# Second block: inverse norms of the keys computed early, and one low weight half carried over a seam of the expert passes

## The chip, the cores and the metric

One core of one Trainium2 chip runs the whole program. The metric is the device time of one execution in microseconds (us), as the median of the runs. A profiled execution of the kernel before stands beside it; all times of single instructions come from that execution and are counted from its first instruction.

## What is computed

Two transformer blocks over 256 tokens of width 1024. The first is not touched. The second normalizes the latent and 256 context tokens, multiplies both by one wide matrix, and feeds three mixers: a gated recurrence ("hgrn"), an RWKV-7 recurrence and a neighbourhood attention. A router then picks experts, and a mixture of 32 experts ends the block. What the change touches is this part of the RWKV mixer and the experts:

```python
def prep(p):
    p = p + (centred_shift(p) - p) * mu
    r, k, v, wdf, wdb, adf, adb, gd = jnp.split(p, list(RWKV_SPLITS), axis=-1)
    kk = hd(k * kk_scale)
    kk = kk / jnp.maximum(jnp.sqrt(jnp.sum(kk * kk, axis=-1, keepdims=True)), 1e-12)
    for d, (wd, ad) in enumerate(((wdf, adf), (wdb, adb))):
        w = -jax.nn.softplus(-(w0[d] + jnp.tanh(wd) @ w_up[d])) - 0.5
        decay = jnp.exp(-jnp.exp(w))
        ...
        dirs.append((hd(decay), hd(k_d), hd(a) * kk))
...
for gi in range(N_GROUPS):
    hid = silu(einsum('nd,edf->nef', h, w_gate[gi])) * einsum('nd,edf->nef', h, w_up[gi])
    y = y + einsum('nef,efd->nd', hid * comb[:, gi, :, None], w_down[gi])
```

## The kernel before

The weights of all large products are split in two parts: ScalarE (ACT) copies a "high" part, VectorE (DVE) subtracts it for the "low" part, and TensorE (PE) does three products for one.

**Second projections.** `second_projections` is one section, with a barrier at each end. Every engine runs one fixed list of instructions, in order. The list comes from generators that yield planned times; `in_turn` always takes the generator with the least planned time (of equals the one named first). The planned times serve only for this order. On the chip an engine runs its list as fast as its semaphores let it.

The input matrix comes in 31 pieces: f (6), vg (4), rw (9, in the order 6, 7, 2, 3, 4, 5, 0, 1, 8), nq, nk and nv (4 each). An f or rw piece gives one unit of output. The four pieces of vg, nq, nk or nv add up to several units, one for each tile of 128 tokens (nq has the tiles 2 and 3 only). The units take PSUM banks 0 to 3 in a ring, in the order of `names`: unit u uses bank u mod 4, and `units.open` makes PE wait until unit u-4 is read out (`units.close`). Four slots hold split pieces, so the high part of piece p waits for the products of piece p-4.

Beside these pieces run nine doubling levels of the hgrn recurrence (`levels_*`, through ACT, DVE, PE and GpSimd (POOL)), then the products that weigh the values (L2707, semaphore `weighed`), the low-rank gates of RWKV (`low_*`, banks 6 and 7), and the keys (`keys_*`). `t_weigh` is the planned time 131.0 of the weighing. In planned times relative to it:

- DVE (`keys_dve`): key times scale and its square (L2480, L2482) at 1.3; four prefix scans (L2488) at 3.6 to 4.2; low part of nv piece 0 at 4.5; the logs of direction 0 (L2498 to L2501) at 4.6 and of direction 1 (L2498 to L2506) at 5.6; low part of nv piece 1 at 10.2; maximum, reciprocal (L2512) and product (L2515) at 10.5 and 11.0; low part of nv piece 2 at 15.9; direction 0's last steps (L2521 to L2527) at 16.0; low part of nv piece 3 at 21.6; direction 1's at 22.0.
- ACT: high part of nv piece 0 at 3.3; square roots of the norms (L2459) at 6.0; copy of nk tile 0 out of PSUM (L197) at 7.3; exponentials of direction 0 (L2464) at 7.5; copy of nk tile 1 at 8.75; high part of nv piece 1 at 9.0; exponentials of direction 1 at 9.5; copies of nk tiles 2 and 3 at 10.2 and 11.6; high parts of nv pieces 2 and 3 at 14.7 and 20.4.
- PE: products of nk piece 3 at 5.6, the two sums over heads (L2443) at 5.7, products of nv piece 0 at 11.3. Its four tiles open the banks of nk's tiles 0 to 3.
- POOL (`keys_pool`): a product for each direction (L2534) once the scaled keys and that direction's exponentials are there.

**Experts.** `passes` handles a number of groups of experts: once with three groups, then once in a loop (`nc.Fori`) for the last group, then a short last stage writes the output. Each call ends with barriers. A pass has 48 halves of weights. `split(i + AHEAD)` makes the parts three halves ahead, so three halves of the next pass are split before the barrier, also after the last pass. The first work of DVE in a pass is `gated_sum` (L4186), whose split feeds the products back to the tokens (L4191) after half 1.

Of the kernel before, what the change touches and what calls it, by code (L numbers as in the profile page):

```python
# [2211 lines left out]
def second_projections(core, I, k, fv, masks, consts, mod, x, X, attended, keys, ycat, coming):  # L2212
# [8 lines left out]
    with ExitStack() as mem, core.section() as sem:  # L2221
# [33 lines left out]
        for name, i, *_ in pieces.rows:  # L2255
            if name in ("f", "rw"):
                names.append((name, i))
            elif i == 0:
                names += [(name, t) for t in tiles[name]]
        units = Units(core, sem, "sec", 4, names)  # L2260
# [142 lines left out]
        def attended_reads(eng, queue, parity):  # L2403
# [8 lines left out]
        up_here, low, low_read, gate_read = sem("up_here"), sem("low"), sem("low_read"), sem("gate_read")  # L2412
        kk_own, kk_summed, kk_rooted, scanned, key_own, key_exp, key_done, key_pool = (sem(n) for n in (
            "kk_own", "kk_summed", "kk_rooted", "scanned", "key_own", "key_exp", "key_done", "key_pool"))
        logs_made, keys_made = (3, 7), 10

# [3 lines left out]
        def low_pe(pe):  # L2420
# [24 lines left out]
        def low_act(act):  # L2445
# [6 lines left out]
            for t in range(TT):  # L2452
                yield t_weigh + 1.5 + 0.05 * t
                act.wait_ge(low, 9 + t)
                nc.scalar.activation(gt[:, t, :], low_bank(t)[:, 0:A_W], ACT.Copy).then_inc(gate_read, 1)
            for hp in range(2):
                yield t_weigh + 6.0 + 0.05 * hp
                act.wait_ge(kk_summed, hp + 1)
                nc.scalar.activation(kn[:, hp], low_bank(hp), ACT.Sqrt).then_inc(kk_rooted, 1)  # L2459
            for d in range(2):  # L2460
# [6 lines left out]
        def keys_dve(dve):  # L2467
# [7 lines left out]

            for hp in range(2):
                yield t_weigh + 1.3 + 0.1 * hp
                dve.wait_ge(weighed, TT)
                units.read(dve, ("rw", 2 + hp))
                V.tensor_scalar(kk[:, hp], X[:, 2 + hp, :], fv["kk_scale"][:, hp:hp + 1], None, ALU.mult).then_inc(kk_own, 1)  # L2480
                dve.wait_ge(kk_own, 2 * hp + 1)
                V.tensor_tensor(kn[:, hp], kk[:, hp], kk[:, hp], ALU.mult).then_inc(kk_own, 1)  # L2482
            for d in range(2):
                for hp in range(2):
                    yield t_weigh + 3.6 + 0.4 * d + 0.2 * hp
                    dve.wait_ge(low_read, 2 * d + hp + 1)
                    dve.wait_ge(out_own, 6)
                    V.tensor_tensor_scan((rt, k2)[d][:, d, hp], consts["chunk_start"], sw[:, d, hp], 0.0, ALU.mult, ALU.add)\  # L2488
                        .then_inc(scanned, 1)
            for d in range(2):  # L2490
                c = [a[:, d].rearrange("p h t -> p (h t)").rearrange("p (c n) -> p c n", n=RW_CHUNK) for a in (kt, k2, rt, sw)]
# [24 lines left out]
            assert own == keys_made  # L2516
            for d in range(2):
# [331 lines left out]
        with nc.Block(no_gpsimd_drain=True) as block:  # L2849
# [23 lines left out]
            @block.scalar  # L2873
            def _(act):
                in_turn(arrived(act), final_act(act), norms[1][2](act), context_act(act), pieces.high_parts(nc, act), bound_act(act), gate_act(act),
                        values_act(act), levels_act(act), shift_act(act), bent_act(act),
                        attended_reads(nc.scalar, act, 1), low_act(act))
# [720 lines left out]
RAW = 4  # L3598
# [542 lines left out]
def experts(core, k, hT, h_tok, weights, tile_d, tile_i, x, g_row, out, m):  # L4141
# [69 lines left out]

    def passes(n_tiles, slots_of, groups_of):

        with core.stage(*names) as (
# [8 lines left out]
            def _(sp):  # L4223
                groups = groups_of(sp)
                sp.dma_start(key[:, :], slots_of(0)).then_inc(key_here, 16)
                for u in range(RAW, n_units):
                    t = u // len(plan)
                    if t and u % len(plan) == RAW:
                        sp.wait_ge(picked, t)
                        sp.dma_start(key[:, :], slots_of(t)).then_inc(key_here, 16)  # L4230
                    if 2 * (u - RAW) + 2 > AHEAD:
                        sp.wait_ge(low, 2 * (u - RAW) + 2 - AHEAD)
                    fetch(sp, u, groups[t]).then_inc(landed[u % RAW], 16)
                for u in range(n_units, n_units + RAW):
                    sp.wait_ge(low, 2 * (u - RAW) + 2 - AHEAD)
                    sp.sem_clear(landed[u % RAW])
                    fetch(sp, u, groups[n_tiles]).then_inc(next_landed[u % RAW] if u % RAW < 2 else landed[u % RAW], 16)

            @block.tensor
            def _(pe):  # L4240
# [9 lines left out]
                for i in range(n_all):  # L4250
                    t, (u, h) = i // n_halves, halves[i % n_halves]
                    kind, e = plan[u]
                    g = PER_GROUP * t + e
                    if i >= AHEAD:
                        pe.wait_ge(low, i + 1 - AHEAD)
                    w = [halved(i, which)[1] for which in range(2)]
# [149 lines left out]
    certain = GROUPS - 1  # L4406
    passes(certain, lambda t: tile_d[t + 1], lambda sp: list(range(GROUPS)))
    tiles = nc.values_load(tile_i[0:1, TILES + 1:TILES + 2], min_val=GROUPS, max_val=TILES)

    with nc.Fori(certain, tiles, 1) as tile:  # L4410
        passes(1, lambda t: tile_d[tile + 1],
               lambda sp: [sp.value_load(tile_i[0:1, bass.ds(tile + n, 1)], min_val=0, max_val=GROUPS - 1) for n in range(2)])

# [283 lines left out]
```

## Time and profile before

| what | value |
|---|---|
| median of 3 runs | 2022.44 us (2021.68 to 2023.82) |
| profiled execution, its own time | 2018.09 us |
| span of that execution, first to last instruction | 2016.3 us |
| PE busy / DVE busy / ACT busy | 91% / 80% / 54% of the span |
| mean granted TensorE clock | 0.97 of full speed |

A busy share is an average over many stages. What matters for one edit is which wait ends last in its own section, so the rows below are mostly from the timeline of the engines in two stretches: 1092 to 1187 us (second half of the second projections) and the two barriers behind the expert passes (1858 to 1862 us and 2004 to 2007 us).

### The profile page before, as it was taken

What the parts mean: (1) busy time and instruction counts of PE and PEld (TensorE: products, weight loads), DVE (VectorE), ACT (ScalarE), POOL (GpSimd) and SP (SyncE); (2) the same over time, 40 slices, a digit from 0 to 9 for tenths busy, and PEclk for the clock granted to TensorE, in tenths of its full rate; (3) what the DMA queues carried; (4) which work ended last, traced back from release to release, by engine and by line L of the source; (5) the groups of instructions that cost most, each with busy time, mean ns of one, the idle gap of its engine ahead of it and who ended that gap; (6) DMA issues with size and microseconds to landing.
All of it is one profiled execution on the core that took longest, in us unless ns stands there. A gap on an engine that the chain in (4) does not pass through costs nothing. (4 is left out here: it accounts for less than half of the span.)

```text
span 2016.3 us, 31666 instructions
## 1 busy us (share of the span) xinstructions
PE 1830.6 (91%) x12866; PEld 1562.5 (77%) x12866; DVE 1610.4 (80%) x2113; ACT 1090.9 (54%) x1316; POOL 145.0 (7%) x151
## 2 busy tenths in 40 slices
PE   2989989998989989999899968997999999999998
PEld 2876769997866769997777657876788788787886
DVE  6778888987788888987579487557888888988887
ACT  2643636653653637562565333125677677776775
POOL 0000000000000000000056047300000000000000
PEclk9989999999999999999999987998899999999999
DMA  7667766656567757556522100006599899898997
GB/s 282 208 222 242 256 226 252 233 205 225 198 217 244 260 189 289 219 196 242 182 83 64 61 12 15 19 16 247 191 372 375 316 377 375 318 373 316 349 381 292
DMA packets 158288, 460.54 MB, mean 228 GB/s; under 512 B 11072, under 2 KB 13760, under 8 KB 155584
## 3 DMA queue, kind: packets, MB, share of 16 engines
q1 hardware_dynamic: 158144, 458.52, 63.7%
q8 instruction: 103, 1.69, 0.3%
q14 instruction: 41, 0.34, 0.1%
HBM read 457.43 MB, written 1.05 MB: 227 GB/s over the span
## 5 line engine op out<-in xcount | busy, mean ns | idle before, releaser
L217 DVE TENSOR_TENSOR me_wlow<-me_w,me_whigh 128x2048 fp32r<-128x2048 f32 (+1 forms) x203 | 451.5, 2247 | 77.5 <-ACT me_whigh L212 77.1
L212 ACT ACTIVATE me_whigh<-me_w 128x2048 fp32r<-128x2048 f32 (+1 forms) x203 | 380.3, 1885 | 116.9 <-PE ps L225 107.2
L223 PE MATMUL ps<-me_whigh,me_xhigh 128*128 128x512 f32 x512 | 204.0, 398 | 5.1 <-PEq L124 3.1
L225 PE MATMUL ps<-me_whigh,me_xlow 128*128 128x512 f32 x528 | 206.9, 392 | 0.0
L223 PE MATMUL ps<-up_xhigh,ffn_whigh 128*128 128x256 f32 x704 | 199.8, 284 | 2.6 <-DVE ffn_wlow L217 1.5
L224 PE MATMUL ps<-me_wlow,me_xhigh 128*128 128x512 f32 x512 | 200.5, 392 | 0.0
L224 PE MATMUL ps<-up_xlow,ffn_whigh 128*128 128x256 f32 x704 | 199.2, 283 | 0.0
L225 PE MATMUL ps<-up_xhigh,ffn_wlow 128*128 128x256 f32 x704 | 199.2, 283 | 0.0
L217 DVE TENSOR_TENSOR ffn_wlow<-ffn_w,ffn_whigh 128x2048 fp32r<-128x2048 f32 (+1 forms) x72 | 149.3, 2110 | 42.4 <-ACT ffn_whigh L212 42.3
L217 DVE TENSOR_TENSOR mix_wlow<-mix_w,mix_whigh 128x1024 fp32r<-128x1024 f32 (+2 forms) x116 | 140.0, 1210 | 21.8 <-ACT mix_whigh L212 21.7
L212 ACT ACTIVATE ffn_whigh<-ffn_w 128x2048 fp32r<-128x2048 f32 (+1 forms) x72 | 123.2, 1760 | 43.1 <-PE ps L225 43.1
L212 ACT ACTIVATE mix_whigh<-mix_w 128x1024 fp32r<-128x1024 f32 (+2 forms) x116 | 120.3, 1047 | 44.0 <-DMA mix_w<-w_mix 22.3
L223 PEld LDWEIGHTS ps<-up_xhigh,ffn_whigh 128*128 128x128 f32 x704 | 135.1, 192 | 3.3 <-issue 3.3
L223 PE MATMUL ps<-mix_whigh,mix_xhigh 128*128 128x512 f32 (+1 forms) x320 | 131.5, 411 | 5.8 <-DVE mix_sq L1717 2.8
L224 PEld LDWEIGHTS ps<-up_xlow,ffn_whigh 128*128 128x128 f32 x704 | 135.1, 192 | 0.0
L225 PEld LDWEIGHTS ps<-up_xhigh,ffn_wlow 128*128 128x128 f32 x704 | 135.1, 192 | 0.0
L224 PE MATMUL ps<-mix_wlow,mix_xhigh 128*128 128x512 f32 (+1 forms) x320 | 125.0, 391 | 0.0
L225 PE MATMUL ps<-mix_whigh,mix_xlow 128*128 128x512 f32 (+1 forms) x320 | 124.8, 390 | 0.0
L485 DVE SCALAR_TENSOR_TENSOR mix_ada_w<-mix_ada_w,mix_ada_row 128x1024 f32<-128x1024 f32 x96 | 116.3, 1216 | 2.0 <-DMA mix_ada_w<-ada_w 2.0
L225 PEld LDWEIGHTS ps<-me_whigh,me_xlow 128*128 128x128 f32 x528 | 99.8, 189 | 21.3
L223 PEld LDWEIGHTS ps<-me_whigh,me_xhigh 128*128 128x128 f32 x512 | 96.9, 189 | 24.8 <-issue 5.6
L224 PEld LDWEIGHTS ps<-me_wlow,me_xhigh 128*128 128x128 f32 x512 | 97.1, 190 | 19.2
(682 smaller groups left out, 4147.8 us busy)
## 6 DMA issues: line engine op xcount, KB each, us to landing
me_w<-w_exp_gate SPq DMA_DIRECT2D x34, 2048.0 KB, 9.8
me_w<-w_exp_up SPq DMA_DIRECT2D x34, 2048.0 KB, 10.3
me_w<-w_exp_down SPq DMA_DIRECT2D x32, 2048.0 KB, 10.4
mix_w<-w_mix SPq DMA_DIRECT2D x108, 512.0 KB, 4.0
mix_ada_w<-ada_w SPq DMA_DIRECT2D x96, 512.0 KB, 4.6
ffn_w<-ffn_w_up SPq DMA_DIRECT2D x20, 2048.0 KB, 7.8
ffn_w<-ffn_w_down SPq DMA_DIRECT2D x8, 2048.0 KB, 8.8
sec_w<-w_in SPq DMA_DIRECT2D x31, 512.0 KB, 3.6
```

The lines of the kernel that those rows point to most:

```text
L212: return nc.scalar.activation(high, x, ACT.Copy)
L217: return nc.vector.tensor_tensor(low, x, high.bitcast(F32), ALU.subtract)
L223: nc.tensor.matmul(out, lh, rh, start=start, stop=False)
L224: nc.tensor.matmul(out, lh, rl, start=False, stop=False)
L225: return nc.tensor.matmul(out, ll, rh, start=False, stop=stop)
L485: nc.vector.scalar_tensor_tensor(out=w, in0=w, scalar=1.0, in1=self.row, op0=ALU.mult, op1=ALU.mult, accum_out=self.sums[:, i:i + 1]).then ...
```

## The change

It moves the norms of the keys. ACT squares the scaled keys once the shifted rows 2 and 3 are there (`norms_act`), into free columns of `ycat` (`key_sq`). PE sums them over heads ahead of nq piece 0, into two new units ("kn", 0) and ("kn", 1) of the ring of banks. ACT copies the sums out and takes the square roots after level 9's exponentials. DVE takes maximum and reciprocal at planned 0.1. Its two scans of direction 0 stand at 1.25 in place of 3.6 and wait for `weighed` only; one instruction per head pair makes the scaled, normalized key at 4.5. Direction 0's logs stay at 4.6, direction 1's go from 5.6 to 10.3. The old sums (PE), roots (ACT) and five DVE steps are gone.

In the experts, a pass carries one low half over its end (`left` = 1) where it carried three. The looped pass starts with one made (`made` = 1): DVE splits half 1 ahead of `gated_sum` and half 2 behind it. The high parts are still made three ahead.

```diff
             elif i == 0:
+                if name == "nq":
+                    names += [("kn", 0), ("kn", 1)]
                 names += [(name, t) for t in tiles[name]]
...
                 yield pieces.at[p]
+                if (name, i) == ("nq", 0):
+                    for hp in range(2):
+                        pe.wait_ge(kk_squared, hp + 1)
+                        nc.tensor.matmul(units.open(pe, ("kn", hp)), consts["head_ones"], key_sq[:, hp],
+                                         start=True, stop=True).then_inc(kk_summed, 1)
...
+        keys_made, logs_made = 4, (7, 11)
+        key_sq = ycat[:, :, A_W:A_W + NTOK]
...
-            for hp in range(2):
-                yield t_weigh + 5.7 + 0.05 * hp
-                pe.wait_ge(kk_own, 4)
-                pe.wait_ge(gate_read, hp + 1)
-                nc.tensor.matmul(low_bank(hp), consts["head_ones"], kn[:, hp], start=True, stop=True).then_inc(kk_summed, 1)
+
+        def norms_act(act):
             for hp in range(2):
+                yield ready_at(("rw", 3)) + 3.4 + 0.1 * hp
+                units.read(act, ("rw", 2 + hp))
+                nc.scalar.activation(key_sq[:, hp], X[:, 2 + hp, :], ACT.Square, scale=fv["kk_scale"][:, hp:hp + 1])\
+                    .then_inc(kk_squared, 1)
+            for hp in range(2):
+                yield pieces.when("nq", 0) + 1.0 + 0.1 * hp
+                act.wait_ge(kk_summed, hp + 1)
+                units.close(nc.scalar.activation(key_sq[:, hp], units.bank(("kn", hp)), ACT.Copy), ("kn", hp))
+            for hp in range(2):
+                yield when(len(SPANS), 2.3 + 0.1 * hp)
+                units.read(act, ("kn", hp))
+                nc.scalar.activation(key_sq[:, hp], key_sq[:, hp], ACT.Sqrt).then_inc(kk_rooted, 1)
...
-            for hp in range(2):
-                yield t_weigh + 1.3 + 0.1 * hp
-                dve.wait_ge(weighed, TT)
-                units.read(dve, ("rw", 2 + hp))
-                V.tensor_scalar(kk[:, hp], X[:, 2 + hp, :], fv["kk_scale"][:, hp:hp + 1], None, ALU.mult).then_inc(kk_own, 1)
-                dve.wait_ge(kk_own, 2 * hp + 1)
-                V.tensor_tensor(kn[:, hp], kk[:, hp], kk[:, hp], ALU.mult).then_inc(kk_own, 1)
+            yield t_weigh + 0.1
+            dve.wait_ge(kk_rooted, 2)
+            mine(V.tensor_scalar(key_sq, key_sq, 1e-12, None, ALU.max))
+            dve.wait_ge(key_own, own)
+            mine(V.reciprocal(key_sq, key_sq))
             for d in range(2):
                 for hp in range(2):
-                    yield t_weigh + 3.6 + 0.4 * d + 0.2 * hp
+                    yield t_weigh + (1.25, 4.0)[d] + 0.2 * hp
                     dve.wait_ge(low_read, 2 * d + hp + 1)
-                    dve.wait_ge(out_own, 6)
+                    if d == 0:
+                        dve.wait_ge(weighed, TT)
+                    else:
+                        dve.wait_ge(out_own, 6)
...
+            yield t_weigh + 4.5
+            dve.wait_ge(key_own, own)
+            dve.wait_ge(weighed, TT)
+            for hp in range(2):
+                units.read(dve, ("rw", 2 + hp))
+                mine(V.scalar_tensor_tensor(out=kk[:, hp], in0=X[:, 2 + hp, :], scalar=fv["kk_scale"][:, hp:hp + 1],
+                                            in1=key_sq[:, hp], op0=ALU.mult, op1=ALU.mult))
...
-                yield t_weigh + 4.6 + 1.0 * d
+                yield t_weigh + (4.6, 10.3)[d]
...
-            yield t_weigh + 10.5
-            dve.wait_ge(kk_rooted, 2)
-            mine(V.tensor_scalar(kn, kn, 1e-12, None, ALU.max))
-            dve.wait_ge(key_own, own)
-            mine(V.reciprocal(kn, kn))
-            yield t_weigh + 11.0
-            dve.wait_ge(key_own, own)
-            mine(V.tensor_tensor(kk, kk, kn, ALU.mult))
...
-    def passes(n_tiles, slots_of, groups_of):
+    def passes(n_tiles, slots_of, groups_of, made, left):
...
                 def split(i):
-                    dve.wait_ge(high, i + 1 - AHEAD)
+                    if i >= n_all + left:
+                        return
+                    if i >= AHEAD:
+                        dve.wait_ge(high, i + 1 - AHEAD)
...
+                for i in range(made, AHEAD - 1):
+                    split(i)
                 for n in range(2):
                     gated_sum(n).then_inc(summed, 1)
+                for i in range(max(made, AHEAD - 1), AHEAD):
+                    split(i)
                 sums_low(0)
```

The waits of PE and SP on `low` count from `made` in place of AHEAD, which names the same halves as before. ACT's two old square roots (L2459) are gone as well.

## Rows read from the trace of the kernel before

**Rows 1.** The page's first line.

```profile
span 2016.3 us, 31666 instructions
```

**Rows 2.** Waits from 1095 to 1190 us: total us, times, longest us.

```profile
DVE sec_small L2797 <- ACT rw_space L2740: 21.4, 1, 21.4
...
PE ps L223 <- DVE sec_wlow L217: 5.7, 2, 2.9
...
PE ps L223 <- ACT na_qk L197: 4.0, 2, 2.1
```

**Rows 3.** Timeline of PE around nq: start us, us, instruction, idle before it.

```profile
1092.34 0.50 PE L223 MATMUL ps<-sec_whigh,sec_xhigh 128*128 128x512 f32 x1
...
1098.02 2.06 PE L2664 MATMUL ps<-rw_space 64*128 64x128 f32 x32
...
1106.47 0.71 PE L2674 MATMUL ps<-rw_space 64*128 64x128 f32 x8 [0.72 <-DVE rw_space L2749]
```

**Rows 4.** Timeline of PE from 1150 us to the section's end.

```profile
1150.54 1.88 PE L2443 MATMUL ps<-rw_space,consts 128*128 128x512 f32 x4
1155.21 0.76 PE L223 MATMUL ps<-sec_whigh,sec_xhigh 128*128 128x512 f32 x1 [2.79 <-DVE sec_wlow L217]
...
1163.80 0.50 PE L223 MATMUL ps<-sec_whigh,sec_xhigh 128*128 128x512 f32 x1 [1.96 <-ACT na_qk L197]
...
1180.64 0.50 PE L223 MATMUL ps<-sec_whigh,sec_xhigh 128*128 128x512 f32 x1 [2.92 <-DVE sec_wlow L217]
```

**Rows 5.** Timeline of DVE.

```profile
1097.36 0.47 DVE L2393 SCALAR_TENSOR_TENSOR rw_x<-ps,sec_small,rw_x 128x255 f32<-128x255 f32 x1
...
1145.18 0.69 DVE L2482 TENSOR_TENSOR rw_space<-rw_space 128x512 f32<-128x512 f32 x1
...
1149.47 4.57 DVE L2488 TENSOR_TENSOR_SCAN rw_space<-consts,rw_space 128x512 f32<-128x512 f32 x4 [0.47 <-DVE ycat L2812]
1153.95 1.20 DVE L217 TENSOR_TENSOR sec_wlow<-sec_w,sec_whigh 128x1024 fp32r<-128x1024 f32 x1
...
1157.42 0.17 DVE L2498 COPY rw_total<-rw_space 128x16 f32<-128x16 f32 x1
...
1162.98 6.55 DVE L2512 RECIPROCAL rw_space<-rw_space 128x1024 f32<-128x1024 f32 x1
...
1171.84 3.42 DVE L2521 TENSOR_TENSOR rw_space<-rw_space 128x1024 f32<-128x1024 f32 x1
...
1180.51 1.22 DVE L2521 TENSOR_TENSOR rw_space<-rw_space 128x1024 f32<-128x1024 f32 x1
```

**Rows 6.** Timeline of ACT.

```profile
1160.03 1.05 ACT L212 ACTIVATE sec_whigh<-sec_w 128x1024 fp32r<-128x1024 f32 x1
1161.16 2.01 ACT L2464 ACTIVATE rw_space<-rw_space 128x1024 f32<-128x1024 f32 x2
...
1163.17 1.06 ACT L197 ACTIVATE na_qk<-ps 128x512 f32<-128x512 f32 x2
```

**Rows 7.** Timeline of POOL.

```profile
1170.87 6.65 POOL L2534 TENSOR_TENSOR rw_space<-rw_space 128x1024 f32<-128x1024 f32 x2 [52.59 <-DVE rw_space L2515]
```

**Rows 8.** Windows: us, busy PE, PEld, DVE, ACT, POOL, clock, DMA.

```profile
1156.00:1158.00 2.00, 2.00 (x5) 1.09 (x4) 2.00 (x4) 0.46 (x1) 0.00 (x0) 0.50 0.00 0
```

**Rows 9.** Timelines of DVE and PE at the seam between the passes.

```profile
1858.09 2.29 DVE L217 TENSOR_TENSOR me_wlow<-me_w,me_whigh 128x2048 fp32r<-128x2048 f32 x1 [0.48 <-ACT me_whigh L212]
1861.87 1.29 DVE L4186 TENSOR_TENSOR h2T<-ps,g_row 128x512 f32<-128x512 f32 x2 [1.49 <-PEq L124]
...
1861.89 0.77 PE L223 MATMUL ps<-me_whigh,me_xhigh 128*128 128x512 f32 x1 [3.13 <-PEq L124]
...
1869.01 0.39 PE L4191 MATMUL ps<-me_yhigh,me_pick_T 128*128 128x512 f32 x1
```

**Rows 10.** The same two timelines at the last stage.

```profile
2006.79 1.29 DVE L4186 TENSOR_TENSOR h2T<-ps,g_row 128x512 f32<-128x512 f32 x2 [1.02 <-PEq L124]
...
2008.93 0.79 PE L4191 MATMUL ps<-me_yhigh,me_pick_T 128*128 128x512 f32 x1 [4.78 <-DVE me_ylow L217]
```

More of the change, by code:

```diff
@@ L2412, in second_projections @@
         up_here, low, low_read, gate_read = sem("up_here"), sem("low"), sem("low_read"), sem("gate_read")
-        kk_own, kk_summed, kk_rooted, scanned, key_own, key_exp, key_done, key_pool = (sem(n) for n in (
-            "kk_own", "kk_summed", "kk_rooted", "scanned", "key_own", "key_exp", "key_done", "key_pool"))
-        logs_made, keys_made = (3, 7), 10
+        kk_squared, kk_summed, kk_rooted, scanned, key_own, key_exp, key_done, key_pool = (sem(n) for n in (
+            "kk_squared", "kk_summed", "kk_rooted", "scanned", "key_own", "key_exp", "key_done", "key_pool"))
+        keys_made, logs_made = 4, (7, 11)
+        key_sq = ycat[:, :, A_W:A_W + NTOK]
         def low_bank(i):
@@ L2455, in low_act @@
                 nc.scalar.activation(gt[:, t, :], low_bank(t)[:, 0:A_W], ACT.Copy).then_inc(gate_read, 1)
-            for hp in range(2):
-                yield t_weigh + 6.0 + 0.05 * hp
-                act.wait_ge(kk_summed, hp + 1)
-                nc.scalar.activation(kn[:, hp], low_bank(hp), ACT.Sqrt).then_inc(kk_rooted, 1)
             for d in range(2):
@@ L2474, in mine @@
                 ins.then_inc(key_own, 1)
-            for hp in range(2):
-                yield t_weigh + 1.3 + 0.1 * hp
-                dve.wait_ge(weighed, TT)
-                units.read(dve, ("rw", 2 + hp))
-                V.tensor_scalar(kk[:, hp], X[:, 2 + hp, :], fv["kk_scale"][:, hp:hp + 1], None, ALU.mult).then_inc(kk_own, 1)
-                dve.wait_ge(kk_own, 2 * hp + 1)
-                V.tensor_tensor(kn[:, hp], kk[:, hp], kk[:, hp], ALU.mult).then_inc(kk_own, 1)
+            yield t_weigh + 0.1
[3 more added lines that the diff above has]
+            mine(V.reciprocal(key_sq, key_sq))
             for d in range(2):
                 for hp in range(2):
-                    yield t_weigh + 3.6 + 0.4 * d + 0.2 * hp
+                    yield t_weigh + (1.25, 4.0)[d] + 0.2 * hp
                     dve.wait_ge(low_read, 2 * d + hp + 1)
-                    dve.wait_ge(out_own, 6)
+                    if d == 0:
+                        dve.wait_ge(weighed, TT)
+                    else:
+                        dve.wait_ge(out_own, 6)
                     V.tensor_tensor_scan((rt, k2)[d][:, d, hp], consts["chunk_start"], sw[:, d, hp], 0.0, ALU.mult, ALU.add)\
                         .then_inc(scanned, 1)
+            yield t_weigh + 4.5
[5 more added lines that the diff above has]
+                                            in1=key_sq[:, hp], op0=ALU.mult, op1=ALU.mult))
+            assert own == keys_made
             for d in range(2):
@@ L2875, in _ @@
                 in_turn(arrived(act), final_act(act), norms[1][2](act), context_act(act), pieces.high_parts(nc, act), bound_act(act), gate_act(act),
-                        values_act(act), levels_act(act), shift_act(act), bent_act(act),
+                        values_act(act), levels_act(act), shift_act(act), bent_act(act), norms_act(act),
                         attended_reads(nc.scalar, act, 1), low_act(act))
@@ L4230, in _ @@
                         sp.dma_start(key[:, :], slots_of(t)).then_inc(key_here, 16)
-                    if 2 * (u - RAW) + 2 > AHEAD:
-                        sp.wait_ge(low, 2 * (u - RAW) + 2 - AHEAD)
+                    if 2 * (u - RAW) + 2 > made:
+                        sp.wait_ge(low, 2 * (u - RAW) + 2 - made)
                     fetch(sp, u, groups[t]).then_inc(landed[u % RAW], 16)
                 for u in range(n_units, n_units + RAW):
-                    sp.wait_ge(low, 2 * (u - RAW) + 2 - AHEAD)
+                    sp.wait_ge(low, 2 * (u - RAW) + 2 - made)
                     sp.sem_clear(landed[u % RAW])
@@ L4253, in _ @@
                     g = PER_GROUP * t + e
-                    if i >= AHEAD:
-                        pe.wait_ge(low, i + 1 - AHEAD)
+                    if i >= made:
+                        pe.wait_ge(low, i + 1 - made)
                     w = [halved(i, which)[1] for which in range(2)]
@@ L4406, in experts @@
     certain = GROUPS - 1
-    passes(certain, lambda t: tile_d[t + 1], lambda sp: list(range(GROUPS)))
+    passes(certain, lambda t: tile_d[t + 1], lambda sp: list(range(GROUPS)), AHEAD, 1)
     tiles = nc.values_load(tile_i[0:1, TILES + 1:TILES + 2], min_val=GROUPS, max_val=TILES)
@@ L4411, in experts @@
         passes(1, lambda t: tile_d[tile + 1],
-               lambda sp: [sp.value_load(tile_i[0:1, bass.ds(tile + n, 1)], min_val=0, max_val=GROUPS - 1) for n in range(2)])
+               lambda sp: [sp.value_load(tile_i[0:1, bass.ds(tile + n, 1)], min_val=0, max_val=GROUPS - 1) for n in range(2)], 1, 1)
     with core.stage("mz_summed", "mz_back", "mz_added", "mz_sum_high", "mz_sum_low", "stored") as (
```

1 line of the change is left out of this document (removed).

## The prediction

> **What bounds the kernel now.** I began with the span [rows 1] and compared it with the execution's own time: 2018.09 - 2016.3 leaves 1.8 us outside the span, which the change does not touch. Then I read the waits of the section that it edits [rows 2]. DVE has one idle time of 21.4 us, until the values are weighed: this is the hole into which maximum and reciprocal go. PE has four waits there, two for low parts from DVE (5.7 us) and two for copies that ACT makes out of PSUM (4.0 us). The question is which of them stand on the path to the section's end, so I went through the timelines.
>
> PE runs without a gap from nq to the old sums, but for 0.72 us [rows 3, 4]. From 1092 to 1150 us PE sets the pace, and what is put into it there comes out at its end. Behind that, nv piece 0 waits for DVE (2.79 us), then nearly as long for each of two banks. The second bank wait ends at 1163.80. From there PE runs through until 1177.72, waits 2.92 us for DVE's last low part, and ends the section [rows 4]. So two chains matter: PE's own work up to the weighing, and then DVE's logs, ACT's exponentials, ACT's bank copies and PE. At both seams of the experts DVE's spare split is what ends last [rows 9, 10].
>
> **Work that is hidden.** The squares on ACT wait for the shifted rows 2 and 3, which the list also has DVE finish ahead of level 5; I cost them at nothing, since the level behind them next waits for PE and POOL. If that cover is gone they cost the four ACT instructions, at 0.53 us each (half of L197's pair in [rows 6]), 2.1 us. The roots stand behind level 9's exponentials, where ACT waits for PE. Maximum and reciprocal (6.55 us alone [rows 5]) fit the 21.4 us with more than 14 us to spare. No DMA is added or moved in this section.
>
> **PE ahead of the weighing.** The sums move from 1150.54, where 2.8 us of waiting follows them, to the front of nq piece 0, where PE has no slack. They cost 1.88 us [rows 4]. Two more units in the ring also change who waits for which bank. Units 10 to 18 are rw's. ("nq", 3) was unit 20 and took the bank of unit 16, (rw, 0), long read. It becomes unit 22 and takes that of unit 18, (rw, 8), the last one shifted. Its reader is the DVE instruction at 1097.36, 0.47 us long [rows 5]. PE gets to tile 3 at 1092.34 + 1.88 + a quarter of the 5.68 us from there to 1098.02 [rows 3] = 1095.6. I take DVE's read to end at 1097.5, 0.3 us early, because the new copies on ACT make POOL's level 7 start later. That is a stall of 1.8 us. The gap of 0.72 us takes some back. Shift at the weighing: 1.88 + 1.8 - 0.72 = **3.0 us**. Bounds: 0, if DVE's side has slack that I miss and the bank is free, and 4.1, if nothing is absorbed and the read ends where it did.
>
> **DVE and ACT behind the weighing.** Gone from DVE are two scalings and two squares (some 2.4 us), maximum and reciprocal (7.2) and the product (1.2). Two instructions of 512 columns are added, at 0.65 us by the 0.69 of L2482 [rows 5]. But the chain that PE waits for is this:
>
> - The second pair of scans starts at 1149.47 + 3.0 = 1152.5 and takes half of 4.57, until 1154.8. The low part of nv 0 and the logs of direction 0 took 1157.42 - 1153.95 = 3.5, and the two new instructions go between: 1159.6.
> - Exponentials of direction 0: 2.1, until 1161.7. Copy of nk tile 1 and high part of nv 1: 0.5 + 1.05, until 1163.2 [rows 6]. DVE has nothing to do meanwhile, because direction 1's logs now stand behind the low part of nv 1, which waits for that high part.
> - POOL's first product (half of 6.65 us, [rows 7]) now starts at 1161.7, since the scaled keys are there early. DVE's product at 1171.84 took 3.42 us where the same one took 1.22 at 1180.51 [rows 5]: it was issued a microsecond behind POOL's first and ended 1.1 us after that had to end. So the low part of nv 1 ends at 1161.7 + 3.3 + 1.2 = 1166.2, and not at 1164.4.
> - Logs of direction 1: from 1157.42 until the exponentials at 1161.16 is 3.7 us, so 1169.9. From there to PE's restart was 1163.80 - 1161.16 = 2.6 [rows 4, 6]: 1172.5, **8.7 us late**.
>
> The Trainium skill (SBUF — State Buffer, Who interferes with whom) says that of a VectorE instruction with two SBUF inputs and a GpSimd one that reads SBUF, the later blocks until the first has ended. The row at 1171.84 agrees. Without the rule the low part would cost 1.2 us and the section 1.8 us less, a net of +2.1 in place of +3.9.
>
> PE has 13.9 us of products from there, then nv 3. Its low part will be ready, because DVE is 9 us shorter, so the wait of 2.92 us is gone. Section: 8.7 - 2.9 = +5.8. Bounds: with the shift at 0 it is +2.8; with all of 4.1 it is +6.9.
>
> **The clock.** PE was idle 2.79 us at 1152, and the stretch 1156 to 1158 shows a granted clock of 0.50, the lower level of 1.2 GHz [rows 8]. Waits of 1.96 us [rows 4] were followed by matmuls at the short spacing. The wait for direction 1 becomes some 8 us, with a single tile of products in the 9 us ahead. I expect the lower level behind it, and take what the six matmuls at 1155.21 lost: they took up to 1158, 2.8 us against 1.4. That is +1.3 (below: 0, as behind the wait of 2.92 us at 1180.64, whose first matmul took 0.50 where a slow one took 0.76; above: 1.7, for a few matmuls more). The Trainium skill (TensorE: Matmul & The Clock Gate, HAM oscillation) says that a wait between groups of products which lasts too long makes the next group start slow. The stretch at 1156 agrees. By that rule the 1.3 us are paid, without it the net is +2.6.
>
> **The seams.** At the first one DVE starts at 1861.87 after 1.49 us of idle, so its last split ended at 1860.38; PE starts at 1861.89 after 3.13, so it ended at 1858.76 [rows 9]. Without two splits of 2.29 us DVE is done before PE, and the barrier moves by 1860.38 - 1858.76 = 1.62 us. Given back? DVE now has one split, two sums, one split and two low sums in front of the products at L4191: 2.2 + 1.2 + 2.2 + 1.3 = 6.9 us from 1860.25, so 1867.2. PE comes there from 1869.01 - 1.62 = 1867.4 on, or earlier at the full clock. Nothing is lost, but 0.2 us is all the slack. SP's next fetch waits for half 1, ready at 1862.5, when its queue would get there anyway. At the end: DVE ended at 2006.79 - 1.02 = 2005.77, PE at 2008.93 - 4.78 = 2004.15 [rows 10], again 1.62. Together **-3.2 us**, between 0 (the barrier waits for something else that ends with DVE) and -4.8 (the restart at the full clock too).
>
> **Sum.** +5.8 + 1.3 - 3.2 = +3.9 us: 2018.09 + 3.9 = 2022.0 by the profiled execution. The median of the runs is 4.35 us above that execution, so the time is 2022.44 + 3.9 = **2026.3 us**.
>
> **Rivals.**
>
> 1. *The shift is not passed on.* PE absorbs the sums and the bank stall ahead of the weighing, and only the later logs count: +2.8 - 3.2 = -0.4, 2022.0 us, no change. For it: DVE and POOL, not PE, set the earlier levels. Against it: 0.72 us of gap in all [rows 3].
> 2. *The shorter DVE list pays, faster.* If direction 1's exponentials start no later than 1161.16, PE's bank waits stay, the wait of 2.92 us for DVE vanishes, and the seams add 3.2: -6.1, 2016.3 us. It decides where ACT reaches nk tile 2's copy by 1163.2. For it: 9 us less on DVE, and a bank copy (nk tile 0) that no longer waits for the old roots. Against it: the order of the list puts a copy, a high part and a low part ahead of those logs.
> 3. *The seams give nothing*, because the barrier was PE's all along: 5.8 + 1.3 = +7.1, 2029.5 us, slower. For it: both waits are released by PE's sequencer [rows 9, 10]. Against it: DVE's work ends 1.6 us later than PE's.
>
> **Chances.** A change of 0.2%, or 4.0 us, is about what a measurement of this kernel can tell from none. Forecast 0.58: its bounds run from +2 to +6 us, so half of it each side of +4.0: 0.30 no change, 0.28 slower. Rival 1: 0.20, 0.18 of it no change and 0.02 slower. Rival 3: 0.12, slower. Rival 2: 0.10, 0.09 faster and 0.01 no change. Faster 0.09, no change 0.49, slower 0.42. The range of 2020.5 to 2029.5 takes in the forecast, rival 1 and most of rival 3; it leaves out rival 2 and the worst of the sums, less than 2 in 10.
>
> **What would show it.** In the new profile: the two sums at 1092.3 and behind them a PE wait of 1.8 us for DVE's L2393; maximum and reciprocal done before 1135; DVE's reduction at 1146.9 in place of 1143.86; DVE idle for 3 to 4 us ahead of nv 1's low part, itself 2 to 3 us long; a PE wait of some 8 us for ACT's L197, with a granted clock of 0.50 behind it; no wait ahead of nv 3; the next section 5 to 7.5 us late; both seams 1.6 us shorter. I am wrong if ACT's copy of nk tile 2 comes before 1166, if PE does not stop at nq tile 3, or if the seams keep their 3.13 and 4.78 us.

## The result, and the profile after

The change made the kernel slower. Ten runs of the kernel after have a median of 2029.21 us, ten of the kernel before, timed with them, 2021.93 us. The ratio is 1.0032 (95% interval 1.0021 to 1.0043), which is +6.5 us (4.2 to 8.7). The profiled execution took 2026.42 us, 8.3 us more than the one of before.

```profile
span 2024.6 us, 31665 instructions
```

Waits of the kernel after from 1085 to 1195 us (total us, times, longest us), beside [rows 2]:

```profile
DVE sec_small L2811 <- ACT rw_space L2754: 14.2, 1, 14.2
PE ps L223 <- ACT na_qk L197: 10.2, 2, 6.4
...
PE ps L223 <- DVE sec_wlow L217: 2.3, 1, 2.3
```

DVE's idle time shrank from 21.4 to 14.2 us, so the reciprocal did go into the hole. PE's two waits for PSUM banks grew from 4.0 to 10.2 us, and one of its two waits for low parts, 2.9 us, is gone. Now PE's timeline, from nq piece 0 through both seams, beside [rows 3, 4, 9, 10]:

```profile
1093.43 1.98 PE L2348 MATMUL ps<-ycat,consts 128*128 128x512 f32 x4
...
1097.39 0.50 PE L223 MATMUL ps<-sec_whigh,sec_xhigh 128*128 128x512 f32 x1 [0.59 <-DVE rw_x L2400]
...
1155.82 0.50 PE L223 MATMUL ps<-sec_whigh,sec_xhigh 128*128 128x512 f32 x1 [2.28 <-DVE sec_wlow L217]
...
1162.13 0.80 PE L223 MATMUL ps<-sec_whigh,sec_xhigh 128*128 128x512 f32 x1 [3.78 <-ACT na_qk L197]
...
1171.48 0.79 PE L223 MATMUL ps<-sec_whigh,sec_xhigh 128*128 128x512 f32 x1 [6.42 <-ACT na_qk L197]
...
1871.65 0.47 PE L223 MATMUL ps<-me_whigh,me_xhigh 128*128 128x512 f32 x1 [1.55 <-PEq L124]
...
1878.59 0.50 PE L4205 MATMUL ps<-me_yhigh,me_pick_T 128*128 128x512 f32 x1 [1.21 <-DVE me_ylow L217]
...
2017.08 0.80 PE L4205 MATMUL ps<-me_yhigh,me_pick_T 128*128 128x512 f32 x1 [3.21 <-DVE me_ylow L217]
```

The sums take 1.98 us ahead of nq, and 0.59 us of waiting follows at tile 3. Behind the weighing PE waits three times for ever longer (2.28, 3.78, 6.42 us), and then not again ahead of nv piece 3. The seams' waits fell from 3.13 to 1.55 and from 4.78 to 3.21 us. Behind the first seam there is a new wait of 1.21 us for DVE's `me_ylow`, where the kernel before had none. DVE's timeline, beside [rows 5]:

```profile
1095.66 0.68 DVE L2762 TENSOR_TENSOR rw_space<-rw_space 128x512 f32<-128x512 f32 x1
1096.26 0.68 DVE L2763 TENSOR_TENSOR rw_space<-rw_space 128x512 f32<-128x512 f32 x1
1096.87 0.47 DVE L2400 SCALAR_TENSOR_TENSOR rw_x<-ps,sec_small,rw_x 128x255 f32<-128x255 f32 x1
...
1125.90 6.55 DVE L2494 RECIPROCAL ycat<-ycat 128x1024 f32<-128x1024 f32 x1
...
1146.70 0.69 DVE L2811 TENSOR_REDUCE sec_small<-rw_space 128x8 f32<-128x512 f32 x1 [14.24 <-ACT rw_space L2754]
...
1163.05 2.13 DVE L217 TENSOR_TENSOR sec_wlow<-sec_w,sec_whigh 128x1024 fp32r<-128x1024 f32 x1 [3.60 <-ACT sec_whigh L212]
1165.11 0.16 DVE L2521 COPY rw_total<-rw_space 128x16 f32<-128x16 f32 x1
```

The reciprocal ends at 1132.45, long before the reduction. DVE then stands idle for 3.60 us in front of the low part of nv piece 1, and the logs of direction 1 wait behind that low part until 1165.11, although their data are ready. ACT and POOL show who waits for whom:

```profile
1161.97 1.04 ACT L212 ACTIVATE sec_whigh<-sec_w 128x1024 fp32r<-128x1024 f32 x1
...
1168.83 2.00 ACT L2478 ACTIVATE rw_space<-rw_space 128x1024 f32<-128x1024 f32 x2 [5.82 <-DVE rw_space L2529]
1170.85 1.06 ACT L197 ACTIVATE na_qk<-ps 128x512 f32<-128x512 f32 x2
...
1193.31 0.60 ACT L197 ACTIVATE na_v<-ps 128x512 f32<-128x512 f32 x1 [0.76 <-PE ps L225]
1195.02 2.00 ACT L3280 ACTIVATE rw_ah<-rw_space 128x1024 f32<-128x1024 f32 x2 [1.12 <-PEq L124]
```

```profile
1096.31 1.77 POOL L2762 TENSOR_TENSOR rw_space<-rw_space 128x512 f32<-128x512 f32 x1 [7.29 <-ACT rw_space L2745]
...
1161.73 2.37 POOL L2548 TENSOR_TENSOR rw_space<-rw_space 128x1024 f32<-128x1024 f32 x1 [40.60 <-ACT rw_total L2479]
```

ACT waits 5.82 us for DVE's logs, makes the exponentials, and only then copies nk's tile 2 out of the bank for which PE waits: 1168.83 + 2.00 = 1170.83, copy until 1171.4, PE on at 1171.48. The low part at 1163.05 was issued while POOL's product ran (1161.73 to 1164.10) and took 2.13 us in place of 1.2. The windows (us, busy PE, PEld, DVE, ACT, POOL, clock, DMA):

```profile
1154.00:1156.00 2.00, 0.18 (x1) 0.18 (x2) 2.00 (x3) 0.00 (x0) 0.00 (x0) 1.00 0.00 0
1158.00:1162.00 4.00, 0.35 (x1) 0.00 (x0) 1.45 (x2) 2.52 (x5) 0.27 (x1) 0.50 0.00 0
1164.00:1171.00 7.00, 1.05 (x3) 0.33 (x1) 4.76 (x5) 2.17 (x4) 0.10 (x1) 0.50 0.00 0
1173.00:1175.00 2.00, 2.00 (x6) 1.57 (x5) 2.00 (x2) 0.80 (x1) 0.39 (x1) 0.50 0.00 0
...
1355.00:1359.00 4.00, 4.00 (x60) 3.43 (x59) 0.62 (x3) 1.04 (x3) 0.00 (x0) 0.50 0.02 4
...
1363.00:1367.00 4.00, 4.00 (x62) 3.13 (x62) 2.85 (x8) 0.00 (x0) 0.00 (x0) 0.81 0.02 4
```

The matmuls behind the 6.42 us run at the lower level of 1.2 GHz. The clock did not fall behind that wait, though: it is at 1.00 until 1156, and 0.58 from 1156 to 1158, so it fell at 1156.3, half a microsecond after PE had come back from the wait of 2.28 us. It then stayed at 0.50 through the waits of 3.78 and 6.42 us until 1176.8 (0.80 from 1176 to 1178).

The last two rows lie in the recurrences, far behind the change. At that place of its own the kernel before shows the upper level:

```profile
1348.00:1352.00 4.00, 3.87 (x98) 2.81 (x90) 1.91 (x6) 0.81 (x3) 0.00 (x0) 1.00 0.02 4
```

PE's row there, of the kernel after and then of the kernel before:

```profile
1354.33 1.11 PE L3412 MATMUL ps<-base,na_ring 128*128 128x128 f32 x4 [1.45 <-ACT na_ring L3457]
```

```profile
1347.07 0.66 PE L3398 MATMUL ps<-base,na_ring 128*128 128x128 f32 x4 [1.45 <-ACT na_ring L3443]
```

Both kernels have the same wait of 1.45 us. In the kernel after the clock falls where it ends (1.00 from 1351 to 1354, 0.50 from 1355), in the kernel before it does not.

**Where the two profiles part.** The section starts 1.1 us later, in code that did not change (960.77, now 961.88; in the thirteen profiles of this study it starts anywhere from 959.3 to 966.8, so the totals of two profiles say little and only their stages are compared). I call *front* the time from there to DVE's reduction, and *late* the time from the reduction to the end of ACT's last copy of nv. Front went from 183.1 to 184.8, late from 43.2 to 47.2; the section is 5.7 us longer. The recurrences (from ACT's first `rw_ah` to the start of DVE's last product with `rw_gate`) went from 186.5 to 190.4 us, and 0.6 us are lost up to the router. The seams give back 1.58 + 0.18 + 1.57 = 3.3 us; the 0.18 is the stretch from the first seam's restart to the products at L4205 (7.12 us before, 6.94 now). Sum: 1.1 + 5.7 + 3.9 + 0.6 - 3.3 = 8.0 of the 8.3.

### The profile page after: what moved, and what is told of

It reads as the page before. It is cut to its first block and busy times, and to the rows that moved or that the text cites. A ratio compares the mean times of both kernels' runs of the same rounds, so it can differ in the third digit from the quotient of the medians.

```text
span 2024.6 us, 31665 instructions
## 1 busy us (share of the span) xinstructions
PE 1838.3 (91%) x12866; PEld 1567.3 (77%) x12866; DVE 1600.8 (79%) x2108; ACT 1094.2 (54%) x1321; POOL 142.5 (7%) x151
## 5 line engine op out<-in xcount | busy, mean ns | idle before, releaser
L217 DVE TENSOR_TENSOR me_wlow<-me_w,me_whigh 128x2048 fp32r<-128x2048 f32 (+1 forms) x201 | 446.6, 2246 | 77.5 <-ACT me_whigh L212 71.9
```

Of the source, the lines that this page charges most:

```text
L217: return nc.vector.tensor_tensor(low, x, high.bitcast(F32), ALU.subtract)
```

## The experiments

The table has the stages of each kernel's one profile, in us. "Low" says whether a stretch at 0.50 shows some 159 to 171 us behind the section's end (the end of ACT's last copy of nv). The last columns set the difference to before that section and seams give (from the profiles) against the timed one, the ratio less 1 times the median of before.

| kernel | front | late | recurrences | low | section and seams | timed, us (95%) |
|---|---|---|---|---|---|---|
| before | 183.1 | 43.2 | 186.5 | no | | |
| after | 184.8 | 47.2 | 190.4 | yes | +2.4 | +6.5 (4.2 to 8.7) |
| seam_only | 183.3 | 43.2 | 185.9 | no | -3.2 | -3.0 (-5.7 to -0.6) |
| keys_only | 187.2 | 47.7 | 191.0 | yes | +8.6 | +7.3 (4.3 to 10.1) |
| logs_early | 186.3 | 44.0 | 190.5 | yes | +0.7 | -0.4 (-3.2 to 2.4) |
| banks_first | 184.8 | 39.7 | 191.4 | yes | -5.1 | -2.0 (-4.9 to 1.0) |
| before_late2 | 183.1 | 43.2 | 187.1 | no | | |
| before_late5 | 184.2 | 43.2 | 184.5 | no | | |
| after_late2 | 184.5 | 47.4 | 189.6 | yes | | |
| after_late5 | 186.0 | 47.6 | 186.1 | no | | |
| before_banks | 184.2 | 43.0 | 189.4 | yes | | |
| sums_at_nk | 184.4 | 46.1 | 186.4 | no | | |
| combo | 186.4 | 38.6 | 187.0 | no | -4.6 | -5.7 (-8.9 to -2.2) |

Front scatters by 2.7 us for the same code: 184.5 to 187.2 in the six profiles that have the new code up to there (after, keys_only, logs_early, banks_first, after_late2, after_late5), mean 185.6, and 183.1 to 184.2 in the five that have the old one, mean 183.6. Late repeats within 0.5 us (47.2 to 47.7) for one code.

**seam_only, keys_only: each half alone.** The first is the kernel before with the new `passes`; the second the kernel after with the old one.

```diff
-    def passes(n_tiles, slots_of, groups_of):
+    def passes(n_tiles, slots_of, groups_of, made, left):
```

> The kernel before with the change to the experts alone. My theory: each of the two barriers comes 1.6 us earlier, so 3.3 us less than the kernel before (ratio 0.9984), with PE idle 1.5 us at the first barrier. Rival (the looped pass gives it back): the products back to the tokens wait for DVE's low sums by more than 1.6 us, and the time does not move.

> The changed kernel with the experts as before. My theory: the keys' part alone costs what the change costs plus 3.3 us, so about 10 us over the kernel before by the timed runs (ratio 1.0048), and 5.8 us of it lie inside the projections' section. Rival (the section costs 5.8 us and nothing else does; what stands beside it in the changed kernel's one profile is scatter of the clock and of transfers): about 6 us, ratio 1.0029.

seam_only had 2019.4 us, ratio 0.9985 (0.9972 to 0.9997); keys_only 2030.26 us, ratio 1.0036 (1.0021 to 1.005). PE at the seams of seam_only:

```profile
1865.27 0.47 PE L223 MATMUL ps<-me_whigh,me_xhigh 128*128 128x512 f32 x1 [1.55 <-PEq L124]
...
1872.20 0.50 PE L4191 MATMUL ps<-me_yhigh,me_pick_T 128*128 128x512 f32 x1 [1.24 <-DVE me_ylow L217]
```

The 1.55 us of the full change stand here too. The seams are worth their 3.3 us (3.0 timed), the keys' half alone costs the time, and the rival in which the seams give nothing is out. For keys_only some 10 us were expected and 6 by the rival; the timed 7.3 us lie between, and their interval (4.3 to 10.1) holds both.

Its profile has a front of 187.2 us, 2.4 more than after, in the same code. Its rows of PE, DVE and POOL, at the place where after has its 0.59 us, show what lengthened it:

```profile
1095.88 0.80 PE L223 MATMUL ps<-sec_whigh,sec_xhigh 128*128 128x512 f32 x1 [3.45 <-DVE rw_x L2400]
```

```profile
1093.69 1.75 DVE L2763 TENSOR_TENSOR rw_space<-rw_space 128x512 f32<-128x512 f32 x1
```

```profile
1093.18 1.71 POOL L2763 TENSOR_TENSOR rw_space<-rw_space 128x512 f32<-128x512 f32 x1
```

Here POOL came first, DVE's product took 1.75 us in place of 0.68, and PE waited 3.45 us for the bank. Of the six profiles with the new front three show 0.59 or 0.60 us there, one 3.45, and two no wait of this kind.

**logs_early: direction 1's logs back at their old place.**

```diff
-                yield t_weigh + (4.6, 10.3)[d]
+                yield t_weigh + (4.6, 5.6)[d]
```

> The changed kernel with the logs of direction 1 back at planned 5.6, ahead of the low part of nv piece 1. My theory: those logs no longer wait for ACT's high part and POOL's product, ACT's exponentials of direction 1 start some 3.4 us earlier, and the time falls by 3 to 3.5 us against the changed kernel. Rival (the sums ahead of nq set the end): no difference from the changed kernel.

2022.93 us, ratio 0.9998 (0.9984 to 1.0012). Late fell from 47.2 to 44.0 us, as the theory had it, and the rival (no difference from after) is out. The timed step from after is larger, about 7 us, but the two were not timed in one series, and their intervals are wide. PE and DVE:

```profile
1164.76 0.79 PE L223 MATMUL ps<-sec_whigh,sec_xhigh 128*128 128x512 f32 x1 [4.31 <-ACT na_qk L197]
...
1170.57 0.79 PE L223 MATMUL ps<-sec_whigh,sec_xhigh 128*128 128x512 f32 x1 [2.88 <-ACT na_qk L197]
```

```profile
1164.48 3.40 DVE L2529 TENSOR_TENSOR rw_space<-rw_space 128x1024 f32<-128x1024 f32 x1
```

The long wait for the bank fell from 6.42 to 2.88 us, the one ahead of it rose from 3.78 to 4.31. The third log product was caught by POOL's product and took 3.40 us in place of 1.2; without that block the wait would probably have been shorter still, which no run here shows.

**banks_first: ACT copies nk out ahead of the exponentials.** If it is the place of the copy on ACT's list that makes PE wait, and not the logs themselves, then this edit removes the wait with the logs left late.

```diff
-                        yield ready_at((name, t))
+                        yield min(ready_at((name, t)), t_weigh + 7.4) if name == "nk" else ready_at((name, t))
```

> The changed kernel with one edit: ACT's copies of all four nk tiles out of PSUM stand ahead of the exponentials of direction 0. My theory (PE waits for a bank copy that is queued behind exponentials which wait for logs): PE's waits of 3.8 and 6.4 us for L197 vanish, a wait of 2 to 3 us for nv 1's low part takes their place, and the section ends 7 to 8 us earlier than in the changed kernel, so some 5 us less than the kernel before. Rival (the lateness of DVE's weighing sets the end): less than 2 us of it are gained.

2020.6 us, ratio 0.999 (0.9976 to 1.0005). PE:

```profile
1153.26 0.50 PE L223 MATMUL ps<-sec_whigh,sec_xhigh 128*128 128x512 f32 x1 [2.28 <-DVE sec_wlow L217]
...
1162.68 0.50 PE L223 MATMUL ps<-sec_whigh,sec_xhigh 128*128 128x512 f32 x1 [2.08 <-DVE sec_wlow L217]
...
1171.99 0.50 PE L223 MATMUL ps<-sec_whigh,sec_xhigh 128*128 128x512 f32 x1 [1.98 <-DVE sec_wlow L217]
```

No wait for L197 is left, and late fell by 7.5 us to 39.7. PE's three waits are 6.3 us in sum, where after has 12.5; the rest is the clock. It fell here too, although each wait's first matmul took 0.50 us: the granted clock is 0.50 from 1154 to 1157 and from 1164 to 1167, but 1.00 from 1158 to 1163 and from 1168 to 1176. With logs_early this settles the mechanism of the 4 us in late: logs, exponentials and the bank copy stand in one chain, and late shrinks when either the logs or the copy is moved. The timed intervals of logs_early and banks_first lie wholly below that of after. But the recurrences took 191.4 us in the profile, and of the 5 us expected against the kernel before the timed runs show 2.0, with an interval that holds zero.

**before_late2, before_late5, after_late2, after_late5: the barrier later, with nothing else changed.** The recurrences behind the section were some 4 us longer in each of the four profiles with the keys' change so far. One theory is that the shift of the barrier sets where TensorE's clock falls, the rival that the new code leaves something behind (other columns, other timing inside). These four add 2 or 5 copies at the end of ACT's list, which ends last.

```diff
+                units.read(act, ("rw", 2))
+                for n in range(2):
+                    nc.scalar.activation(xs[0][:, n, :], X[:, 2, :], ACT.Copy)
```

> The kernel before with two idle copies on ACT (0.5 us each) behind its last copy, so that the barrier of the projections comes 1.1 us later and nothing else changes. Question: the stage behind (from the last copy of nv to the router) took 236.0 us in the kernel before and 240.5 to 242.8 us in the four kernels with the keys' change, with a granted clock of 0.50 some 162 to 170 us into it. My theory (the clock's rise and fall depend on where PE's work lies in time, and the change moved it): the same stage takes 236 us at some shifts and 240 us at others, in either kernel. Rival (something of the keys' change itself, its tile or its order, slows that stage): 236 plus the 1.1 us here, whatever the shift.

> The kernel before with five such copies, 2.7 us. Theory: the stage behind takes the 2.7 us more, and a further 3 to 4 us if the low clock falls into the last steps of the recurrences. Rival: 236 plus 2.7 us.

> The changed kernel with two such copies, 1.1 us. Theory: if this shift moves the low clock out of the last steps of the recurrences the stage falls to some 237 us; one of the two shifts should. Rival: 240.5 plus 1.1 us.

> The changed kernel with five such copies, 2.7 us. Theory: as for two copies; at one of the two shifts the stretch of clock 0.50 at 162 to 170 us is gone. Rival: 240.5 plus 2.7 us, with the stretch where it was.

Times 2020.89, 2024.6, 2023.84 and 2028.75 us. From the last copy of nv to ACT's first `rw_ah` it is 1.12 us without the copies, 2.14 with two and 3.70 with five, so the barrier came 1.0 and 2.6 us later. after_late5 has the code of after and not its low stretch:

```profile
1356.00:1360.00 4.00, 2.55 (x27) 1.59 (x27) 1.72 (x5) 1.12 (x4) 0.00 (x0) 1.00 0.10 33
1360.00:1364.00 4.00, 4.00 (x92) 2.92 (x93) 1.49 (x6) 1.24 (x4) 0.00 (x0) 1.00 0.02 6
```

Its recurrences took 186.1 us. So the keys' code alone does not force the stretch. Neither kernel before showed it when delayed, so a later barrier alone does not bring it either. With one run for each, whether the delay or the single execution made the difference is not shown.

**before_banks: the bank edit in the kernel before.** Does the stretch need the keys' change? And is the bank order alone enough for the gain?

> The kernel before with only the four copies of nk ahead of the exponentials. My theory: PE's two waits for L197 vanish but the section ends where it did (43.2 us behind the reduction), because nv 3 still waits for DVE's last low part; the shorter DVE list and the early copies pay only together. Rival (the bank waits alone are worth their 4 us): the section ends 4 us earlier.

A single run, 2028.37 us. PE:

```profile
1162.37 0.80 PE L223 MATMUL ps<-sec_whigh,sec_xhigh 128*128 128x512 f32 x1 [2.79 <-DVE sec_wlow L217]
...
1179.06 0.55 PE L223 MATMUL ps<-sec_whigh,sec_xhigh 128*128 128x512 f32 x1 [3.85 <-DVE sec_wlow L217]
...
1187.69 0.50 PE L223 MATMUL ps<-sec_whigh,sec_xhigh 128*128 128x512 f32 x1 [1.28 <-DVE sec_wlow L217]
```

The waits for L197 are gone here too, but with the old norms on DVE its low parts come late instead (7.9 us in all), and late is 43.0, no better than before. So the rival (a section 4 us shorter) is out, and the bank order pays only together with the shorter DVE list. And the low stretch shows in a kernel without any of the keys' change (189.4 us).

**sums_at_nk: the two sums ahead of nk, in place of nq.**

```diff
-                if name == "nq":
+                if name == "nk":
                     names += [("kn", 0), ("kn", 1)]
...
-                if (name, i) == ("nq", 0):
+                if (name, i) == ("nk", 0):
...
-                yield pieces.when("nq", 0) + 1.0 + 0.1 * hp
+                yield pieces.when("nk", 0) + 1.0 + 0.1 * hp
```

> The changed kernel with the sums, their two units and ACT's copies of them ahead of nk piece 0. My theory: PE's wait of 0.6 us for the bank of (rw, 8) vanishes and DVE's reduction comes some 0.6 us earlier in the section (184.2 us from its start in place of 184.8), no more, because the two sums still cost PE 2 us. Rival (PE has room for the sums there): 183.1 us, as in the kernel before.

A single run, 2019.1 us. PE:

```profile
1097.48 2.06 PE L2678 MATMUL ps<-rw_space 64*128 64x128 f32 x32 [0.55 <-DVE rw_space L2763]
...
1106.41 0.71 PE L2688 MATMUL ps<-rw_space 64*128 64x128 f32 x8 [1.19 <-DVE rw_space L2763]
```

The bank stall of 0.59 us is gone, but PE now waits 0.55 and 1.19 us for DVE's level products: ahead of nq part of the sums' time had only filled these waits. Front is 184.4 (184.2 expected, 183.1 by the rival), not distinguishable from the 184.5 to 187.2 with the sums ahead of nq. Late is 46.1, 1.1 us under after: PE comes back from the same wait of 6.42 us at 1170.25, and the clock is at 0.50 for 2.9 us from there, where in after it is for 5.3.

**combo: banks_first, logs_early and sums_at_nk together, with the seams.**

> The changed kernel with three edits: the four copies of nk ahead of the exponentials, direction 1's logs at planned 5.6, and the sums over heads ahead of nk piece 0 in place of nq piece 0. My theory: the section takes 221 to 222 us, against 224.5 with the copies alone and 226.3 in the kernel before; with the seams' 3.3 us and the low clock of the recurrences where it is (some 4 us back) the time lies 3 to 4 us under the kernel before, ratio 0.998 to 0.9985. Rival (PE is the bound once the banks are free): the section stays at 224.5 us.

2017.49 us, ratio 0.9972 (0.9956 to 0.9989): faster than before, and the lowest ratio of the study (0.998 to 0.9985 expected). PE and DVE:

```profile
1157.26 0.50 PE L223 MATMUL ps<-sec_whigh,sec_xhigh 128*128 128x512 f32 x1 [2.27 <-DVE sec_wlow L217]
...
1167.88 0.50 PE L223 MATMUL ps<-sec_whigh,sec_xhigh 128*128 128x512 f32 x1 [3.29 <-DVE sec_wlow L217]
```

```profile
1163.29 3.40 DVE L2529 TENSOR_TENSOR rw_space<-rw_space 128x1024 f32<-128x1024 f32 x1
```

Late is 38.6 and the section 225.0 us, 1.3 shorter than before. The section was expected at 221 to 222 us, and 225.0 is the rival's number (224.5, PE as the bound). But PE waits 2.27 and 3.29 us here, both times for DVE. Of the missing 3 to 4 us, 2 lie in the front (186.4, where sums_at_nk has 184.4) and the rest in late. There a log product issued just behind POOL's start costs 3.40 us once more, and the low part of nv piece 1 stands behind it (1166.61). The recurrences took 187.0 us, without the low stretch that was expected in them.

## Why the prediction was right or wrong

The time lies in the range (2029.2, upper end 2029.5), near its edge. The sum of +3.9 us was too small by 2.6, and the likelier side of the 0.2% was missed: no change had 0.49, slower 0.42. That the range held is in part luck: the shift and the chain were taken too large, and a term that is not in the sum at all made up for it.

**The sums and the stall ahead of the weighing: too large.** The sums cost 1.98 us (1.88 said). In the profile of after PE did stop at nq tile 3 for L2400, but for 0.59 us, not 1.8. The step that failed there is that this read ends 0.3 us earlier. It ended at 1097.34 (before: 1097.36 + 0.47 = 1097.83), in a section that began 1.1 us later, so 1.6 us earlier by the section's clock. These are DVE's two products ahead of that read in the kernel before, and one of POOL's:

```profile
1094.60 1.14 DVE L2748 TENSOR_TENSOR rw_space<-rw_space 128x512 f32<-128x512 f32 x1
1095.66 1.77 DVE L2749 TENSOR_TENSOR rw_space<-rw_space 128x512 f32<-128x512 f32 x1
```

```profile
1095.14 1.74 POOL L2749 TENSOR_TENSOR rw_space<-rw_space 128x512 f32<-128x512 f32 x1
```

The second was issued behind POOL's start and ran until POOL's end was past. Now POOL's starts at 1096.31, DVE comes first, and each of the two takes 0.68 us. But this is no fixed gain: in keys_only, with the same code, POOL came first again and the stall was 3.45 us. The forecast let POOL start later, but not so late that DVE comes first, and the stall hangs on this order: with DVE first it was 0 to 0.6 us. The shift at the reduction is 184.8 - 183.1 = 1.7 us (3.0 said); by the means of the six and the five profiles it is 2.0, with a scatter of 2.7 in the new front.

**Maximum, reciprocal, squares, roots: right.** All hidden: PE's sums start at 1093.43 without a wait for the squares, and 14.2 us of DVE's idle time are left.

**The chain behind the weighing: right in kind, 2.1 us too large.** Counted from the section's start, PE reached tile 2 at 203.0 us before and at 209.6 now, 6.6 late where 8.7 was said. 1.3 of the difference is the smaller shift. Most of the rest is POOL's product: alone it takes 2.37 us, not the 3.3 that I took as half of a pair between which DVE ran. The block of DVE by POOL was there, 2.13 us against 1.2. The wait of 2.92 us ahead of nv 3 vanished, as said. banks_first and logs_early show the links of the copy and of the logs.

**The clock: 2.1 us, 1.3 said.** From PE's restart at tile 2 to the last copy's end are now 22.42 us, where 23.25 - 2.92 = 20.33 would be expected. The 0.79 us of the first matmul and the 0.50 of the windows at 1164 and 1173 carry it; two tiles of products were slow (1171.5 to 1176.8), not one. The reason given was wrong in one point: the clock had been low since 1156.3 and had not risen again, so it was not the long wait that brought it down. The section in all: +5.7 us, +7.1 said.

**The seams: right.** -3.3 us in the profile (-3.2 said), and -3.0 timed in seam_only. The slack of 0.2 us behind the first seam was used up: the clock was 1.00 behind the restart (1871 to 1874; 0.50 from 1862 to 1865 in the kernel before), PE came to the products at L4205 sooner, and waited 1.21 us there for DVE. So what the faster clock could have given was not gained.

**The term that I had not.** Section and seams make +2.4 us, less than the forecast. The profile has 3.9 us more in the recurrences, where nothing was edited. Three of them lie in the low stretch at 1355. The step that failed is that the prediction took the work behind the barrier to be only moved, and had no term for it. after_late5 and before_banks show that the stretch comes and goes in kernels of either kind: 189.4 to 191.4 us with it, 184.5 to 187.1 without.

How much of the timed 6.5 us this term holds is open. In the table, section and seams alone meet the timed interval for seam_only, keys_only, logs_early and combo, and lie just outside for banks_first. For after they fall short by at least 1.8 us. With the mean fronts in place of the single ones after stands at some +2.7, still short by 1.5. That fits the ten runs' mean granted clock, 0.963, where the twelve of each other timed kernel have 0.965 to 0.967 and those of the kernel before that were timed with these 0.966 (of the ten timed with after no clock is on record). The runs of one kernel differ too: of the kernel before one took 2017.5 us at a mean clock of 0.971, another 2029.2 us at 0.964. A stretch in every timed execution of a kernel whose profile shows it, and in none of the kernel before, does not fit either: by the profiles' recurrences keys_only would then stand at 8.6 + 4.5 = +13.1 us and logs_early at 0.7 + 4.0 = +4.7, both above their intervals (up to 10.1 and 2.4). So the single execution seems to have its part in it. How large that part is against the shift of the barrier would need several profiles of one kernel.

**The rivals.** The shift not passed on (+2.8 for the section): no, the front moved by 1.7 us (2.0 by the means), late grew by 4, and the section by 5.7. The shorter DVE list paying: no in the change as made, since the order of the list kept the logs behind a low part; but logs_early, banks_first and combo show that this was only the order, and that the shorter list is worth 4.6 us of late (38.6 against 43.2) once ACT's copies and DVE's logs stand right. The seams giving nothing: no.

## What to carry to other kernels

When work is taken off an engine with a fixed order, look at what now stands in front of the next instruction that another engine waits for: here 9 us of work went from DVE's list behind the weighing and PE still waited 6.2 us longer for banks, because a log stood behind a low part and a bank copy behind the exponentials of those logs. Put the copies that free a producer's banks ahead of work that has slack. An edit of 2 us in one stage is judged by that stage's length in the profile, because here the clock elsewhere added or took 4 us in the total; take more than one profile before a story is built on such a stretch, or on a stage that scatters as the front did.

## What was unexpected of the hardware

The granted clock fell behind short waits, and not behind all of them. In the recurrences it fell at the end of a wait of 1.45 us (1354.33) and was 0.50 while PE was busy for 4.00 of 4.00 us (1355 to 1359); the same wait in the kernel before (1347.07) was followed by 1.00. In the section it fell half a microsecond behind a wait of 2.28 us, and stayed low through those of 3.78 and 6.42 us; in banks_first it fell behind waits of 2.28 and 2.08 us and not behind one of 1.98, and in the kernel before not behind that of 2.92. The Trainium skill (TensorE: Matmul & The Clock Gate, HAM oscillation) tells of waits between groups of products, and every fall named here stands behind such a wait; which waits bring the clock down no run here shows. A first matmul of 0.50 us doesn't prove a high clock either: the fall can come just behind it.

The same DVE product of 128x512 took 0.68 us where DVE came first, and 1.14 and 1.77 us behind a POOL product; one of 128x1024 took 3.40 us when issued 0.11 us behind POOL's start (1163.18 in combo). The Trainium skill (SBUF — State Buffer, Who interferes with whom) says that the later of the two blocks until the first has ended, and these rows agree.
